# A two-layer decoder with a mixture of experts in fp32: sums of x and of the scatters kept in PSUM, 21 weight slots, smaller last transfers

## The reference, cut to what matters

```python
D_MODEL, SEQ, DEPTH = 1024, 256, 2          # all float32, batch 1
for l in range(DEPTH):
    h = rms_norm(x, norm1_g[l])
    proj = h @ w_in[l]                      # (256, 3072): q, k, v of two kinds of attention
    o_da = ...                              # differential attention, 4 heads of 128
    o_sb = ...                              # stick-breaking attention, 8 heads of 64
    x = x + concatenate([o_da, o_sb]) @ w_out[l]
    h2 = rms_norm(x, norm2_g[l])
    # router: best of 4 groups, in it the best 2 of 8 experts -> combine (256, 32)
    hg = einsum('sd,edf->sef', h2, w_gate[l])    # 32 experts, d 1024, f 256
    hu = einsum('sd,edf->sef', h2, w_up[l])
    act = silu(hg) * hu * combine[..., None]
    x = x + einsum('sef,efd->sd', act, w_down[l])
```

## Time and profile before

| | us |
|---|---|
| median of 3 runs (lowest, highest) | 745.71 (744.35, 745.98) |
| the profiled execution's own time | 742.31 |
| its span, first to last instruction | 740.5 |
| TensorE busy | 652.9 (88%) |
| VectorE busy | 305.3 (41%) |
| ScalarE busy | 119.0 (16%) |
| moved by the DMA engines | 239.09 MB, mean 323 GB/s |

### The profile page before, as it was taken

One profiled execution on the slowest core, in us unless ns is written; L12 is line 12 of the kernel. 1 busy time (PEld: TensorE's weight loads), 2 busy tenths in 40 slices (PEclk: granted clock), 3 DMA queues, 4 the chain that ended last, 5 costly groups with the idle time before them and its releaser, 6 DMA issues.

```text
span 740.5 us, 12416 instructions
## 1 busy us (share of the span) xinstructions
PE 652.9 (88%) x4796; PEld 374.1 (51%) x4797; DVE 305.3 (41%) x625; ACT 119.0 (16%) x284; POOL 9.0 (1%) x19
## 2 busy tenths in 40 slices
PE   7999999988798897784999999999898979785966
PEld 4478555475554353432345864546644535443522
DVE  0445663164353443431424377422633434432413
ACT  3103442220000000000031035324000000000000
POOL 0002000000000000000020000000000000000000
PEclk9999999999999998987999999999999999987989
DMA  8798426537999999999999630395299999999995
GB/s 307 264 335 304 169 113 277 234 115 295 415 422 416 393 423 421 421 422 423 388 357 395 271 144 28 129 382 222 67 377 420 422 421 423 422 423 420 423 406 208
DMA packets 52967, 239.09 MB, mean 323 GB/s; under 512 B 7824, under 2 KB 8112, under 8 KB 29376
## 3 DMA queue, kind: packets, MB, share of 16 engines
q1 hardware_dynamic: 52432, 238.14, 80.6%
q0 software_dynamic: 496, 0.44, 0.5%
HBM read 237.51 MB, written 1.05 MB: 322 GB/s over the span
## 4 chain that ended last, share of the span: by engine, by line
PE 67%; DMA 19%; DVE 5%; issue 4%; SPq 2%; DVEq 2%; ACT 1%; ACTq 0%
DMA wbuf<-in_w_down 18%; PE bank L1207 13%; PE bank L1398 11%; PE bank L1366 8%; PE bank L1197 8%; PE bank L1310 7%; PE bank L1410 5%; PE bank L1341 5%; PE bank L1377 2%; DMA wbuf<-in_w_in 1%; SPq L371 1%; PE bank L1266 1%; PE bank L1317 1%; PE bank L1240 1%; PE bank L1286 1%
## 5 line engine op out<-in xcount | busy, mean ns | idle before, releaser
L1398 PE MATMUL bank<-wbuf,qkT 128*32 128x512 f32 x512 | 73.2, 708 | 53.3 <-DMA wbuf<-in_w_down 46.5
L1207 PE MATMUL bank<-wbuf,hTbuf 128*128 128x512 f32 x256 | 114.7, 603 | 3.9 <-DMA wbuf<-in_w_in 3.5
L1366 PE MATMUL bank<-wbuf,qkT 128*32 128x256 f32 x2048 | 113.8, 380 | 2.2 <-DVE qkT L880 2.2
L1366 PEld LDWEIGHTS bank<-wbuf,qkT 128*32 128x32 f32 x2048 | 65.2, 110 | 54.2 <-issue 10.6
L1207 PEld LDWEIGHTS bank<-wbuf,hTbuf 128*128 128x128 f32 x256 | 48.3, 192 | 63.0 <-issue 58.9
L1341 PE MATMUL bank<-qkT,xn 128*128 128x128 f32 x512 | 62.9, 282 | 11.3 <-issue 10.4
L916 DVE TENSOR_TENSOR x_sb<-x_sb,bank 128x512 f32<-128x512 f32 x72 | 49.5, 688 | 51.0 <-PE bank L1410 51.0
L1341 PEld LDWEIGHTS bank<-qkT,xn 128*128 128x128 f32 x512 | 59.9, 196 | 18.4 <-issue 18.4
L1398 PEld LDWEIGHTS bank<-wbuf,qkT 128*32 128x32 f32 x512 | 19.2, 126 | 97.0 <-issue 86.9
L1197 PE MATMUL bank<-hTbuf,wbuf 128*128 128x256 f32 x256 | 56.5, 380 | 0.0
L1310 PE MATMUL bank<-wbuf,hTbuf 128*128 128x512 f32 x128 | 56.1, 594 | 0.0
(11 more groups left out here) (218 smaller groups left out, 564.5 us busy)
## 6 DMA issues: line engine op xcount, KB each, us to landing
wbuf<-in_w_gate SPq DMA_DIRECT2D x64, 1024.0 KB, 14.9
wbuf<-in_w_up SPq DMA_DIRECT2D x64, 1024.0 KB, 17.7
wbuf<-in_w_down SPq DMA_DIRECT2D x56, 1024.0 KB, 14.6
wbuf<-in_w_in SPq DMA_DIRECT2D x24, 1024.0 KB, 14.7
wbuf<-in_w_out SPq DMA_DIRECT2D x8, 1024.0 KB, 6.3
wbuf<-in_w_down SPq DMA_DIRECT2D x16, 512.0 KB, 7.8
x_sb<-in_x SPq DMA_DIRECT2D x2, 512.0 KB, 6.3
out<-x_sb SPq DMA_DIRECT2D x2, 512.0 KB, 2.6
```

The lines of the kernel that those rows point to most:

```text
L1207: last = MM(ps[PROJ_BANK[i][t]][:, :], hT[:, k, t * P:(t + 1) * P], block_rows(i, k), start=(k == 0), stop=(k == KC - 1))
L1366: last = MM(ps[bank][j * SLOTS:(j + 1) * SLOTS, 0:FF], hgT[:, k, j * SLOTS:(j + 1) * SLOTS], halves[:, at[j], k, :], start=(k == 0), stop= ...
L1398: last = MM(ps[banks[h]][j * SLOTS:(j + 1) * SLOTS, :], src[:, c, j * SLOTS:(j + 1) * SLOTS], at[j][:, c * D + h * HALF:c * D + (h + 1) * ...
```

## The change

Parts, in the order in which the kernel comes to them:
- **Start.** The first half block of w_in, one transfer with four k, is four transfers with a semaphore each (`load_start`).
- **Space.** `xn` and `hTbuf` are gone as tiles. Their room becomes slots 19 and 20 of `wbuf`: slot 19 serves attention as `xa` and then set 1's fourth up, slot 20 serves as hT and then set 1's first down. Both are issued by `load_first_sets`. Odd sets' first downs have slot 20 of their own from then on, with a semaphore by parity (`dn0_in`). The normed x is written over x in `x_sb`.
- **x in PSUM.** Before the ranks TensorE multiplies x by the identity into banks 4 to 7 (`keep_x`), in place of twelve `keep_clock` matmuls, and all scatters of the layer accumulate onto it. `into_x`, `x_moe` and `x_more` go. After the last set VectorE and ScalarE copy the four banks to `x_sb`. ScalarE writes the normed x to a spare tile and copies it over x after `keep_x`.
- **Router.** x is transposed by halves as they come (`transpose_half`); the router's weights and gain are laid out by halves of the rows. The first gathered half is evicted by VectorE before the sorting, the second by ScalarE, and TensorE no longer waits for `routed` before its first set.
- **Banks.** All else uses banks 0 to 3; transposed weights go to bank 1, and the second half of the gather waits until they are copied. The weights' transposes of a set move from its predecessor to behind its own ups.
- **Order of loads.** All four ups of g+1 right after the gates (for the last set behind the downs), then three downs of g and the first of g+1. `gate_used` is signalled before ScalarE's exponential.
- **Odd sets' second output half** in two quarters of 256 columns, the first into bank 3, the second into bank 2 once its former half is evicted (`down_quarters`); scatters by quarters, written twice under an If, once with signals for the last set.
- **Last downs.** First halves of three experts, then their second halves by halves of rows: c=0 of all three, c=1 of all three.
- **The loop's place.** In layer 1's second projection TensorE increments an unused semaphore 8 times before each of 16 matmuls (`place_loop`).

```diff
-SLOTS_W = 19
+SLOTS_W = 21
-UP_SLOT = [[4, 5, SLOT_STAGE, 9], [6, 7, 8, 9]]
-DOWN_SLOT = [10, 11, SLOT_VALUES, 16]
+UP_SLOT = [[4, 5, SLOT_STAGE, 9], [6, 7, 8, SLOT_XN]]
+DOWN_SLOT = [[10, 11, SLOT_VALUES, 16], [SLOT_HT, 11, SLOT_VALUES, 16]]
...
+            def load_start():
+                src = w_in[0, :, ORDER[0] * HALF:(ORDER[0] + 1) * HALF].rearrange("(p k) c -> p k c", p=P)
+                dst = slot(BLOCK_SLOT[0][0]).rearrange("p (k c) -> p k c", c=HALF)
+                for k in range(KC // 2):
+                    sp_.dma_start(dst[:, k, :], src[:, k, :]).then_inc(start_in[k], 16)
...
+                sp_.wait_ge(oT_ps, (l + 1) * TT)
+                load_up(l, 1, 3)
...
+                sp_.wait_ge(lg_ps, (l + 1) * TT)
+                load_down(l, 1, 0)
...
-                    if g > 1:
-                        sp_.wait_ge(up_used, l * SETS + g)
-                        load_up(l, g, LANES - 1)
                     if g + 1 < SETS:
                         sp_.wait_ge(gate_used, l * SETS + g)
                         for j in range(LANES):
                             load_gate(l, g + 1, j)
-                    if g == 1:
+                    if g + 1 < SETS - 1:
                         sp_.wait_ge(up_used, l * SETS + g)
-                        load_up(l, g, LANES - 1)
+                        for j in range(LANES):
+                            load_up(l, g + 1, j)
                     sp_.wait_ge(dn_used, l * SETS + g)
                     if g + 1 < SETS:
-                        for j in range(LANES):
+                        for j in range(1, LANES):
                             load_down(l, g, j)
-                        for j in range(LANES - 1):
-                            load_up(l, g + 1, j)
+                        load_down(l, g + 1, 0)
+                        if g + 1 == SETS - 1:
+                            sp_.wait_ge(up_used, l * SETS + g)
+                            for j in range(LANES):
+                                load_up(l, g + 1, j)
                     else:
-                        for h in range(2):
-                            for j in range(LANES):
-                                load_down_half(l, g, j, h)
+                        for j in range(1, LANES):
+                            load_down_half(l, g, j)
+                        for c in range(FC):
+                            for j in range(1, LANES):
+                                load_down_rows(l, g, j, c)
...
+            def normed_to_x(l, t):
+                act.wait_ge(x_kept, l * TT + t + 1)
+                nc.scalar.copy(xn[:, t, :, :], xn_first[t]).then_inc(xn_ready, 1)
...
-                    V.tensor_tensor(x_sb[:, t, c], x_sb[:, t, c], ps[SC_BANK[t][h]][:, :], ALU.add)
...
+            def place_loop(n):
+                for _ in range(n):
+                    pe.sem_inc(placed, 1)
...
+                    if l > 0 and i == 1:
+                        place_loop(8)
...
+            def keep_x(t):
+                for h in range(2):
+                    last = MM(ps[X_BANK[t][h]][:, :], ident, x_sb[:, t, h * HALF:(h + 1) * HALF], start=True, stop=False)
+                last.then_inc(x_kept, 1)
...
+            def down_quarters(l, n, pair, src, second_half):
+                for c in range(FC):
+                    pe.wait_ge(last_dn_in[c], second_half)
+                    for q, (bank, done) in enumerate(((1, first["dn1_ps"]), (0, dn_rest_ps))):
+                        if q == 1 and c == 0:
+                            pe.wait_ge(first["y_d"], n)
+                        for j in range(LANES):
+                            at = slot(DOWN_SLOT[1][j])[:, c * D + HALF + q * QUARTER:c * D + HALF + (q + 1) * QUARTER]
+                            last = MM(ps[DN_BANK[bank]][j * SLOTS:(j + 1) * SLOTS, 0:QUARTER],
+                                      src[:, c, j * SLOTS:(j + 1) * SLOTS], at, start=(c == 0), stop=(c == FC - 1))
+                            if c == FC - 1:
+                                last.then_inc(done, 1)
...
+            def scatter(s, n, weights):
+                for h in range(2):
+                    pe.wait_ge(s["y_a" if h else "y_d"], n)
+                    for t in range(TT):
+                        MM(ps[X_BANK[t][h]][:, :], weights[:, t, :], y[:, h * HALF:(h + 1) * HALF], start=False, stop=False)
```

More of the change, by code:

```diff
@@ L1337, in gather @@
-            def gather(s, n, sel=sel):
+                MM(ps[3][:, 0:EXPERTS], ones, asg[:, TT, :], start=True, stop=True).then_inc(total_ps, 1)
+            def gather(s, n, weights_out=None, sel=sel):
                 pe.wait_ge(s["sel_ready"], n)
                 for k in range(KC):
+                    if k == KC // 2 and weights_out is not None:
+                        pe.wait_ge(first["selwT_out"], weights_out)
                     for t in range(TT):
-                        last = MM(ps[k // 4][:, (k % 4) * P:(k % 4 + 1) * P], xn[:, t, k * P:(k + 1) * P], sel[:, t, :],
+                        last = MM(ps[k // 4][:, (k % 4) * P:(k % 4 + 1) * P], xn[:, t, k, :], sel[:, t, :],
@@ L1388, in transpose_act @@
                 last.then_inc(s["actT_ps"], 1)
-            def down(s, n, banks, src, second_half=None):
-                pe.wait_ge(s["actT_out"], n)
-                at = [slot(DOWN_SLOT[j]) for j in range(LANES)]
-                for h in range(2):
-                    if h == 1 and second_half is not None:
-                        pe.wait_ge(last_dn_in, second_half)
-                    for c in range(FC):
-                        for j in range(LANES):
-                            last = MM(ps[banks[h]][j * SLOTS:(j + 1) * SLOTS, :], src[:, c, j * SLOTS:(j + 1) * SLOTS],
-                                      at[j][:, c * D + h * HALF:c * D + (h + 1) * HALF], start=(c == 0), stop=(c == FC - 1))
-                            if c == FC - 1:
-                                last.then_inc(s[f"dn{h}_ps"], 1)
@@ L1403, in scatter, with down @@
[L1403 to L1411 removed]
+            def down(s, n, parity, src, h, second_half=None):
+                if h == 1 and second_half is not None:
+                    for c in range(FC):
+                        pe.wait_ge(last_dn_in[c], second_half)
+                at = [slot(DOWN_SLOT[parity][j]) for j in range(LANES)]
+                for c in range(FC):
+                    for j in range(LANES):
+                        last = MM(ps[DN_BANK[h]][j * SLOTS:(j + 1) * SLOTS, :], src[:, c, j * SLOTS:(j + 1) * SLOTS],
+                                  at[j][:, c * D + h * HALF:c * D + (h + 1) * HALF], start=(c == 0), stop=(c == FC - 1))
+                        if c == FC - 1:
+                            last.then_inc(s[f"dn{h}_ps"], 1)
@@ new lines, in scatter_quarters @@
+            def scatter_quarters(l, n, pair, last):
+                pe.wait_ge(first["y_d"], n)
+                for t in range(TT):
+                    mm = MM(ps[X_BANK[t][0]][:, :], selwT[:, t, :], y[:, 0:HALF], start=False, stop=last)
+                    if last:
+                        mm.then_inc(x_ps[t][0], 1)
+                pe.wait_ge(first["y_a"], n)
+                for t in range(TT):
+                    for q in range(2):
+                        if t == 0 and q == 1:
+                            pe.wait_ge(y_rest, pair + (l * SETS // 2 + 1))
+                        c = slice(q * QUARTER, (q + 1) * QUARTER)
+                        mm = MM(ps[X_BANK[t][1]][:, c], selwT[:, t, :], y[:, HALF + q * QUARTER:HALF + (q + 1) * QUARTER],
+                                start=False, stop=last and q == 1)
+                    if last:
+                        mm.then_inc(x_ps[t][1], 1)
@@ L1542, in _ @@
                 router(l, 1, 1)
-                keep_clock(12)
+                for t in range(TT):
+                    keep_x(t)
                 ranks(l)
```

396 lines of the change are left out of this document (216 added, 180 removed).

## The result

The changed kernel takes 749.95 us (median of 17 runs, 746.20 to 754.36) beside 744.44 for the kernel before (17 runs, 740.08 to 746.13): ratio 1.0078, 95% interval 1.0057 to 1.0098. It is slower by 0.8%; 725.5 had been forecast.

A forecast was written before the change was run, and what follows sets the result against it. Expert stages were taken to last as long as their weight stream plus what comes before and behind it. Start 2.2 plus two layers of routing 1.2 and expert stage 7.8 gave 20.2 us off 745.71: 725.5, range 718 to 736.

The forecast's parts named there:

- the rival of the other side: Expert loop, lengthened, is fetched anew each pass: 40 us a layer, 806 us; decides from 8 us a pass; chance 0.05.
- Start: First w_in block in four transfers lets the first projection matmuls begin sooner: 2.2 us, bounds 0 and 3.
- Routing: Between attention and experts, earlier router work and earlier eviction of the gathered half: 1.2 us a layer, bounds 0 and 1.9.
- Expert stage: From first gate matmul to last scatter, 208.6 becomes 200.8: 7.8 us a layer, bounds 4.4 and 10.
- the 5.0 of the early loads: Set 1's fourth up and first down, 2 MB, loaded before routing ends while the queue is silent: 5.0 us.
- Edits costed at nothing: Quarters' eviction waits, shared PSUM banks, counter steps and three more parameter loads a layer: all taken as hidden, 0.
- quarters and shared banks: Odd sets' quarters wait 0.6 us a set, hidden by w_down waits; shared banks hidden too; quarters uncovered, 2.4 a layer.
- The 128 steps: Counter steps in layer 1's second projection, 44 to 68 ns each, hidden beside matmuls: 0; uncovered, 5.6 to 8.7 us.
- TensorE's sequencer starves the stream: Rival: first-pass fetch stalls or uncovered steps take back 3.4 a layer and up to 8.7 once: 732 to 736; chance 0.12.
- Sum: Whole kernel: 2.2 + 2 x (1.2 + 7.8) = 20.2 us gained, giving 725.5 from a median of 745.71.
- What was to show it wrong: Bandwidth under 400 GB/s inside an expert stage, instruction packets well above 25, or layer 1's projections outlasting layer 0's.

The follow-up runs named there:

- e7: Changed kernel, 128 steps kept, odd sets' second output half in one piece instead of quarters (down and scatter): 725.5 us, ratio 0.9737 to the kernel before.
- e1: Changed kernel with 96 counter steps ahead of layer 1's loop instead of 128: 726.24 us, ratio 0.9787 to the kernel before.
- e12: Changed kernel with 112 counter steps ahead of layer 1's loop instead of 128: 726.58 us, ratio 0.9767 to the kernel before.
- e6: Changed kernel with 96 steps, VectorE's wait for gains and lambdas moved below `diag_ready`: 722.81 us, ratio 0.9706 to the kernel before.
- e5: Changed kernel with 96 steps, set 1's fourth up and first down issued behind set 2's gates, not early: 736.0 us, ratio 0.9897 to the kernel before.
- e10: Changed kernel with 192 counter steps ahead of layer 1's loop instead of 128: 783.68 us, ratio 1.0545 to the kernel before.
- e2: Changed kernel with no counter steps ahead of layer 1's loop instead of 128: 772.91 us, ratio 1.0411 to the kernel before.

## Why the prediction was wrong

**The step that failed** is the argument against the rival of the other side, "the loop no longer stays with TensorE", which had 0.05: "the two blocks added are a few dozen instructions". They are 49 (e7), the loop grew by 55 in all, and that was no reason: whether the loop stays depends on its start as well, which the other edits move too (174 without any step, where the kernel before has 240). I counted neither the loop nor its start, although a part of the change is named "the loop's place", and I took the 2,048 instructions of the whole store as what a loop may fill. The rival's mechanism was right and its size was not: it forecast four passes fetched anew in both layers and 40 us a layer; in fact layer 0's loop stays, three passes are fetched, and the one layer loses 23.8. The 34.2 us more of issue waits are some 11 for each of the three passes, above the 8 from which the rival was to decide. 725.5 + 23.8 = 749.3, against 749.95 measured. With the mechanism taken away and nothing else (e1, e12) the kernels take 726.24 and 726.58, so the rest of the sum stands, to about 3 us (below).

**Start** (2.2 us). Mis-sized. The first w_in matmul begins at 8.38 instead of 10.32, as said, and its eight take 3.67 us instead of 5.40. But the next projection begins only 1.2 us sooner, at 26.19 against 27.39 in TensorE's timeline of before. The same of the kernel after:

```profile
8.38 3.67 PE L1257 MATMUL bank<-wbuf 128*128 128x512 f32 x8 [1.34 <-ACT wbuf L557]
...
25.69 0.67 PE L1268 MATMUL bank<-wbuf,cst 128*128 128x256 f32 x2 [2.40 <-DVEq L1024]
26.19 4.03 PE L1257 MATMUL bank<-wbuf 128*128 128x512 f32 x9
```

And a line of its chain of waits:

```profile
12.37 12.57 DMA lamv<-in_lambda_k
```

TensorE now waits 2.40 us for VectorE, which waits for the lambdas, a small load that lands at 24.94 (12.37 + 12.57). I had not asked what is late next once the start was shorter; e6 shows that this was it.

**Routing** (1.2 a layer). The stage of layer 0 begins at 162.57, 2.85 sooner than before; 1.2 of it is the start's, 1.7 the routing's. Between the stages in layer 1 (366.14 to 516.50, from first projection matmul to first gate) 150.4 us pass; before, from 376.29 to 528.09, 151.8: 1.4. A little more than forecast, inside its bounds.

**Expert stage** (7.8 a layer). Measured 7.6 in layer 0 and, where the loop stays, 8.2 in layer 1 (208.7 - 200.5), each from one execution of either kernel. e5 confirms the 5.0 of the early loads. **Edits costed at nothing**: quarters and shared banks, right (e7). The 128 steps, right by a wrong working: 44 to 68 ns a step were taken from the earlier trace rows, a row of another operation whose largest was 174; it is about 150 ns, and not the matmul beside them but the sequencer's lead covers them, to its end. "TensorE's sequencer starves the stream" as priced does not occur where the loop stays: issue waits are 7.2 us in e1's stage, 4.9 before. The sum of that rival was wrong as well: 11.5 is 20.2 less the 8.7 of the steps, not the gain without the start's, and with both of its prices only 4.7 are left, which is 741.0 and outside the range.

**Sum.** 1.2 + 1.7 + 1.4 + 7.6 + 8.2 = 20.1 without the fetches, beside 20.2 forecast: each term within 1.0, the errors cancelling. That it comes so near is luck, as a stage of one kernel differs by up to 4 us between executions. Of e1's own span 19.0 us are gone (721.5 beside 740.5), as its copies of the four banks behind the last scatter take 0.4 more than the addition did, the transposes between the layers 0.3, and its layer 0 begins 0.5 later than the kernel's after. By medians it is 17.1 (743.3 in its own comparison), since e1's traced execution is the fastest of its four, 2.9 us under their median, and that of the kernel before only 1.0 under 743.3. The forecast's 725.5 came out near e1's 726.24 because it set out from 745.71, higher than any later median of the kernel before. The range of 718 to 736 was made of the bounds of these terms, and held nothing of the rival that came true, which it put at 806. What was to show it wrong did: holes, 50 packets where "well above 25" was the mark.

## What to carry to other kernels

Before adding a line to a loop that nearly fills TensorE's instruction store, count the compiled loop and where it starts: here 16 instructions ahead of it decided between 726.6 and 750.0 us, and the instruction queue's packets in the profile (23 or 50) told it at a glance. Give a layout that depends on the start a margin on both sides, or shorten the loop, as leaving out the worthless quarters did. When a wait is taken from the head of a chain, look for the next load that lands late.

## What the runs showed of the hardware

- Loops of 1,645 to 1,701 instructions stay with TensorE if they touch seven blocks of 256 and are fetched in each later pass if they touch eight (blocks counted with the fitted 46 to 61). A pass fetches nine packets of 16 KB on average, and in the kernel after stalls for 5.3 to 5.5 us at its head.
- Filler instructions are not free by being short: a semaphore increment took about 150 ns on TensorE's sequencer, 16 x 8 of them were hidden by its lead of some 5 us, 16 x 12 cost 11.0 us and 16 x 19 cost 28.5.
- TensorE's granted clock was lower behind such stalls (0.84 in the 10 us behind one of 5.3). In layer 1's stage it averages 0.95 in e1, 0.95 in the kernel after, 0.90 in e10 and 0.88 in e2, and the same 1,821 matmuls take 170.2, 177.1, 189.0 and 185.8 us, so the average alone does not give their time.
